# Neighbourhood heads: each block of 64 queries against its own 128 keys, its values gathered by 16 transfers from GpSimd

## The reference

```
ncb = GRID_W // NA_COL_BLOCK                        # 4 blocks of 16 columns
kstart = clip(arange(ncb) * 16 - 8, 0, 64 - 32)     # 0, 8, 24, 32
kcol = kstart[:, None] + arange(32)                 # 32 key columns for each block
wstart = clip(qcol - 8, 0, 64 - 16)
col_valid = (kcol >= wstart) & (kcol < wstart + 16)
sc = einsum('bnqhd,banchd->bhnqac', qb, kb) * scale + bias
sc = where(col_valid, sc, -inf)
p = softmax(sc, axis=(-2, -1))
o = einsum('bhnqac,banchd->bnqhd', p, vb)
```

## Time and profile before

| | us |
|---|---|
| median of 3 | 1472.59 (1472.44 to 1472.97) |
| profiled execution | 1472.36 |
| its span | 1471.1 |
| TensorE products busy | 1449.6 |
| VectorE busy | 1043.9 |
| ScalarE busy | 815.8 |
| GpSimd busy | 62.4 |

### The profile page before, as it was taken

The page is one execution under the profiler, slowest core; times in us unless marked ns, Lnnn a source line. Parts: engine busy times, 40 slices in busy tenths (PEclk is TensorE's granted clock), DMA queues, the critical chain, the costliest instruction groups (busy, mean ns, idle before and its releaser), DMA issues.

```text
span 1471.1 us, 19474 instructions
## 1 busy us (share of the span) xinstructions
PE 1449.6 (99%) x7635; PEld 1215.1 (83%) x7635; DVE 1043.9 (71%) x1409; ACT 815.8 (55%) x1159; POOL 62.4 (4%) x100
## 2 busy tenths in 40 slices
PE   7999999999999999999999999999999999999998
PEld 5788887888888788887888888788888888888887
DVE  5656885865567656786866555877988868788886
ACT  3565654444544455754445444686665557775563
POOL 2000000000000000000010000210000012000000
PEclk9999999999999999999999999999999999999999
DMA  9553643566566535543666665336556635356651
GB/s 322 182 162 127 237 169 115 191 229 200 172 193 207 194 103 183 186 139 125 196 203 201 198 202 201 115 115 208 169 196 198 225 119 172 125 182 201 200 181 58
DMA packets 167324, 261.08 MB, mean 177 GB/s; under 512 B 8768, under 2 KB 106720, under 8 KB 166720
## 3 DMA queue, kind: packets, MB, share of 16 engines
q1 hardware_dynamic: 166048, 252.03, 52.0%
q0 software_dynamic: 896, 6.74, 1.2%
q10 hardware_dynamic: 288, 1.05, 0.2%
HBM read 258.74 MB, written 1.05 MB: 177 GB/s over the span
## 4 chain that ended last, share of the span: by engine, by line
PE 85%; DVE 9%; ACT 3%; issue 1%; POOL 1%; DMA 1%; SPq 0%; DVEq 0%; ACTq 0%
PE ps L421 16%; PE ps L492 10%; PE ps L494 10%; PE ps L493 10%; PE ps L422 9%; PE ps L391 6%; PE ps L395 6%; PE ps L393 6%; DVE wlo L1581 3%; PE ps L424 2%; PE ps L546 1%; PE ps L559 1%; PE ps L569 1%; PE ps L449 1%; DVE x L1600 1%
## 5 line engine op out<-in xcount | busy, mean ns | idle before, releaser
L1581 DVE TENSOR_TENSOR wlo<-raw,whi 128x2048 fp32r<-128x2048 f32 (+1 forms) x238 | 528.3, 2229 | 224.7 <-ACT whi L1097 224.7
L1097 ACT ACTIVATE whi<-raw 128x2048 fp32r<-128x2048 f32 (+1 forms) x238 | 441.9, 1866 | 152.2 <-PE ps L494 54.3
L421 PE MATMUL ps<-xT,whi 128*128 128x512 f32 x1008 | 356.4, 395 | 0.0
L422 PE MATMUL ps<-xT,wlo 128*128 128x256 f32 x1152 | 311.2, 280 | 0.0
L492 PE MATMUL ps<-whi,xT 128*128 128x512 f32 (+3 forms) x640 | 250.6, 391 | 4.3 <-DVE xT L1619 2.3
L494 PE MATMUL ps<-whi,xT 128*128 128x512 f32 (+3 forms) x640 | 242.0, 378 | 0.0
L493 PE MATMUL ps<-wlo,xT 128*128 128x512 f32 (+3 forms) x640 | 241.4, 377 | 0.0
L421 PEld LDWEIGHTS ps<-xT,whi 128*128 128x128 f32 x1008 | 189.0, 188 | 42.2
L422 PEld LDWEIGHTS ps<-xT,wlo 128*128 128x128 f32 x1152 | 217.4, 189 | 6.1
L492 PEld LDWEIGHTS ps<-whi,xT 128*128 128x128 f32 x640 | 120.4, 188 | 29.9 <-issue 7.8
L494 PEld LDWEIGHTS ps<-whi,xT 128*128 128x128 f32 x640 | 120.2, 188 | 22.6
(11 more groups left out here) (220 smaller groups left out, 1962.0 us busy)
## 6 DMA issues: line engine op xcount, KB each, us to landing
raw<-in_w_in SPq DMA_DIRECT2D x124, 512.0 KB, 4.7
raw<-in_w_ffn_in SPq DMA_DIRECT2D x88, 512.0 KB, 4.9
raw<-in_w_up SPq DMA_DIRECT2D x88, 512.0 KB, 4.8
raw<-in_w_ffn_out SPq DMA_DIRECT2D x44, 512.0 KB, 4.4
raw<-in_w_down SPq DMA_DIRECT2D x44, 512.0 KB, 4.4
raw<-in_w_branch SPq DMA_DIRECT2D x24, 512.0 KB, 4.6
raw<-in_w_out SPq DMA_DIRECT2D x16, 512.0 KB, 4.5
raw<-in_w_o SPq DMA_DIRECT2D x16, 512.0 KB, 4.7
```

What stands on the lines that cost most here:

```text
L421: PE.matmul(ps[:, b, :], hi, m.xT[:, kt], start=kt == 0, stop=False)
L422: mm = PE.matmul(ps[:, b, 0:S], lo, m.xTh[:, kt], start=False, stop=False)
L1097: AC.activation(m.whi[:, i % SPLIT, 0:w], m.raw[:, slot, 0:w], ACT.Copy).then_inc(s.w_hi, 1)
L1581: DV.tensor_tensor(m.wlo[:, i % SPLIT, 0:w], m.raw[:, slot, 0:w], m.whi[:, i % SPLIT, 0:w].bitcast(F32), ALU.subtract).then_inc(s.w_lo, 1)
```

## The change

Queries and keys are put in another order, so that the 64 queries of one block are neighbours, and each block is scored against its own 128 keys. The scores of a head are then 2 x 128 columns in place of 2 x 256. The queries are reordered when they are copied out of PSUM, the keys are picked by an access pattern, and the bias is laid out to fit on the host: `rpb` holds 128 columns for each half and head, 1 MB in rows of 128 elements. In the free half of `rpb` four tiles of values are put together, one for each block: 16 transfers from SBUF to SBUF, which GpSimd starts once the values are out of PSUM. TensorE waits for them ahead of the first product with values. The results are put back in the order of the tokens when they are copied out.

```
+WINDOWS = (0, 8, 24, 32)
...
     def load_bias(L):
-        PO.dma_start(m.rpb[:], t["rpb"][L]).then_inc(s.lay, 16)
+        PO.dma_start(m.rpb[:, :, :, 0:P], t["rpb"][L]).then_inc(s.lay, 16)
...
         PO.dma_start(m.vec[:], t["b_gate"][L:L + 1, 0:2 * D].broadcast_to([P, 2 * D])).then_inc(s.gate_b, 16)
+        for th in range(2):
+            bank, nth = k.bank[(1, L, "n", 2), th]
+            PO.wait_ge(k.free[bank], nth)
+        for w, k0 in enumerate(WINDOWS):
+            for r in range(4):
+                p0 = r % 2 * 64 + k0
+                PO.dma_start(m.rpb[32 * r:32 * r + 32, 2 * w:2 * w + 2, :, P:S],
+                             m.proj[p0:p0 + 32, r // 2, 1024:1536].rearrange("p (a b e) -> p a b e", a=2, b=2)).then_inc(s.windows_in, 16)
...
+    def score_windows(g0, h0, g):
+        PE.wait_ge(s.qk_out, g0 + g + 1)
+        if h0 + g:
+            PE.wait_ge(s.exped, h0 + 2 * g)
+        for w, k0 in enumerate(WINDOWS):
+            half, b = w // 2, w % 2
+            for j in range(2):
+                qk = m.qk[64 * j:64 * j + 64, g % 2, :]
+                keys = qk[:, S:2 * S].rearrange("p (r c) -> p r c", r=4)[:, :, k0:k0 + 32]
+                mm = PE.matmul(ps[64 * b:64 * b + 64, 3 + j, half * P:(half + 1) * P], qk[:, w * 64:w * 64 + 64], keys,
+                               start=True, stop=True)
+                if w == 3:
+                    mm.then_inc(s.scored, 1)
+    def turn_windows(p0, i, buf):
...
+        for half in range(2):
+            mm = PE.transpose(ps[:, 5, half * P:(half + 1) * P], m.prob[:, buf, half, 0:P], m.ident[:])
+        mm.then_inc(s.probs_turned, 1)
+    def mix_windows(p0, m0, g):
...
+        for w in range(4):
+            for j in range(2):
+                values = m.rpb[:, 2 * w + g // 2, g % 2, P + 64 * j:P + 64 * j + 64]
+                o = (g % 2) * S + 64 * w
+                mm = PE.matmul(ps[64 * j:64 * j + 64, 7, o:o + 64], values, m.probT[:, j, 64 * w:64 * w + 64],
+                               start=True, stop=True)
+        mm.then_inc(s.pairs_mixed, 1)
...
             if g == 1:
-                out_of_psum((1, L, "n", 2))
+                PE.wait_ge(s.windows_in, 256 * (L + 1))
             if g:
-                mix_pair(p0, m0, g - 1, 1024)
+                mix_windows(p0, m0, g - 1)
...
-        AC.activation(m.probT[:, i % 2, :], ps[:, 5, :], ACT.Copy).then_inc(s.probs_out, 1)
+        AC.activation(m.probT[:, i % 2, 0:width], ps[:, 5, 0:width], ACT.Copy).then_inc(s.probs_out, 1)
...
+    def qk_by_columns(buf):
+        DV.wait_ge(s.qk_turned, n.up("groups"))
+        DV.tensor_copy(columns(m.qk[:, buf, 0:S]), by_columns(ps[:, 6, 0:S]))
+        DV.tensor_copy(m.qk[:, buf, S:2 * S], ps[:, 6, S:2 * S]).then_inc(s.qk_out, 1)
...
-                b = DV.tensor_tensor_reduce(m.prob[:, h % 4, th, :], ps[:, 3 + h % 2, th * S:(th + 1) * S], m.rpb[:, h, th, :], 1.0,
+                b = DV.tensor_tensor_reduce(m.prob[:, h % 4, th, 0:P], ps[:, 3 + h % 2, th * P:(th + 1) * P], m.rpb[:, h, th, 0:P], 1.0,
```

More of the change, by code:

```diff
@@ L60 @@
     "gate_tanh", "merged",
-    "rotated", "subln", "lam", "lam_exp",
+    "windows_in", "rotated", "subln", "lam", "lam_exp",
     "qk_turned", "qk_out", "scored", "negm", "exped", "heads_out",
@@ L121, in gemm_names, with by_columns, columns @@
     return seq
+def by_columns(ap):
+    return ap.rearrange("p (r w c) -> p w r c", r=4, w=4)
+def columns(ap):
+    return ap.rearrange("p (w r c) -> p w r c", r=4, w=4)
 def spread(ap, shape, axis=1):
@@ L549, in score_pair @@
                     mm.then_inc(s.scored, 1)
+    def score_windows(g0, h0, g):
[12 more added lines that the diff above has]
+    def turn_windows(p0, i, buf):
+        PE.wait_ge(s.probs_in, p0 + i + 1)
+        if p0 + i:
+            PE.wait_ge(s.probs_out, p0 + i)
+        for half in range(2):
+            mm = PE.transpose(ps[:, 5, half * P:(half + 1) * P], m.prob[:, buf, half, 0:P], m.ident[:])
+        mm.then_inc(s.probs_turned, 1)
+    def mix_windows(p0, m0, g):
+        PE.wait_ge(s.probs_out, p0 + 2 * g + 2)
+        if m0 + g:
+            PE.wait_ge(s.pair_out, m0 + g)
+        for w in range(4):
[5 more added lines that the diff above has]
+        mm.then_inc(s.pairs_mixed, 1)
     def turn_probs(p0, i, buf):
@@ L640, in tensor_program @@
             if g < 4:
-                score_pair(g0, h0, g)
+                score_windows(g0, h0, g)
             if g < 3:
@@ L645, in tensor_program @@
             if g:
-                turn_probs(p0, 2 * g - 2, (2 * g - 2) % 4)
+                turn_windows(p0, 2 * g - 2, (2 * g - 2) % 4)
             fill(g, 2)
             if g:
-                turn_probs(p0, 2 * g - 1, (2 * g - 1) % 4)
+                turn_windows(p0, 2 * g - 1, (2 * g - 1) % 4)
             fill(g, 3)
             if g == 1:
-                out_of_psum((1, L, "n", 2))
+                PE.wait_ge(s.windows_in, 256 * (L + 1))
             if g:
-                mix_pair(p0, m0, g - 1, 1024)
+                mix_windows(p0, m0, g - 1)
         fill(5, 0, rest=True)
@@ L1206, in exp_pair, with probs_out @@
             for th in range(2):
-                src = m.prob[:, h % 4, th, :] if biased else ps[:, 3 + h % 2, th * S:(th + 1) * S]
-                e = AC.activation(m.prob[:, h % 4, th, :], src, ACT.Exp, bias=m.negm[:, h % 4, 1, th:th + 1], scale=scale,
+                dst = m.prob[:, h % 4, th, 0:P if biased else S]
+                src = dst if biased else ps[:, 3 + h % 2, th * S:(th + 1) * S]
+                e = AC.activation(dst, src, ACT.Exp, bias=m.negm[:, h % 4, 1, th:th + 1], scale=scale,
                                   accum_out=m.rs[:, h, th:th + 1])
             e.then_inc(s.exped, 1)
-    def probs_out(p0, i, m_free):
+    def probs_out(p0, i, m_free, width=2 * S):
         AC.wait_ge(s.probs_turned, p0 + i + 1)
@@ L1220, in pair_hi, with windows_hi @@
         AC.activation(m.aTh[:, g, :], ps[:, 7, (g % 2) * S:(g % 2 + 1) * S], ACT.Copy).then_inc(s.pair_hi, 1)
+    def windows_hi(m0, g):
+        AC.wait_ge(s.pairs_mixed, m0 + g + 1)
+        AC.activation(by_columns(m.aTh[:, g, :]), columns(ps[:, 7, (g % 2) * S:(g % 2 + 1) * S]), ACT.Copy).then_inc(s.pair_hi, 1)
     def outputs_hi(kts, bank):
@@ L1275, in scalar_program @@
             if g:
-                probs_out(p0, 2 * g - 2, m0 + g - 1)
+                probs_out(p0, 2 * g - 2, m0 + g - 1, S)
             catch(1, L, "na", g, 2, ahead=SPLIT - (g > 2))
             if g:
-                probs_out(p0, 2 * g - 1, m0 + g - 1)
+                probs_out(p0, 2 * g - 1, m0 + g - 1, S)
             catch(1, L, "na", g, 3)
             if g:
-                pair_hi(m0, g - 1)
+                windows_hi(m0, g - 1)
         catch(1, L, "na", 5, 0)
@@ L1763, in biased_maxima, with normalise_pair @@
             DV.tensor_scalar(m.negm[:, h % 4, 1, :], m.negm[:, h % 4, 0, :], -1.0, None, ALU.mult).then_inc(s.negm, 1)
-    def normalise_pair(h0, g):
+    def normalise_pair(h0, g, width=S):
         DV.wait_ge(s.exped, h0 + 2 * g + 2)
@@ L1769, in normalise_pair @@
             for th in range(2):
-                p = m.prob[:, h % 4, th, :]
+                p = m.prob[:, h % 4, th, 0:width]
                 a = DV.tensor_scalar(p, p, m.ri[:, h, th:th + 1], None, ALU.mult)
@@ L1789, in pair_lo, with windows_lo @@
                          ALU.subtract).then_inc(s.pair_out, 1)
+    def windows_lo(g):
+        DV.wait_ge(s.pair_hi, n.up("pair_hi"))
+        DV.tensor_tensor(by_columns(m.aTl[:, g, :]), columns(ps[:, 7, (g % 2) * S:(g % 2 + 1) * S]),
+                         by_columns(m.aTh[:, g, :].bitcast(F32)), ALU.subtract).then_inc(s.pair_out, 1)
     def blocks_lo(lo, hi, nkt, bank0, koff=0, gain=None):
@@ L1852, in vector_program @@
         h0, p0 = n.up("heads", 8) - 8, n.up("probs", 8) - 8
-        qk_out(P, 0)
+        qk_by_columns(0)
         catch(1, L, "na", 0, 0, ahead=SPLIT - 1)
@@ L1856, in vector_program @@
             if g in (1, 2, 3):
-                normalise_pair(h0, g - 1)
+                normalise_pair(h0, g - 1, P)
             if g < 4:
@@ L1860, in vector_program @@
             if g < 3:
-                qk_out(P, (g + 1) % 2)
+                qk_by_columns((g + 1) % 2)
             catch(1, L, "na", g, 1, ahead=0 if g else SPLIT)
             if g == 3:
-                normalise_pair(h0, g)
+                normalise_pair(h0, g, P)
             if g == 1:
@@ L1873, in vector_program @@
             if g:
-                pair_lo(g - 1)
+                windows_lo(g - 1)
         catch(1, L, "na", 5, 0)
@@ L2262, in rpb_rows @@
     a = np.where(inside[None, None, None, :, None, :], a, np.float32(-1e30))
-    return a.reshape(DEPTH, 8, 2, P, S).transpose(0, 3, 1, 2, 4)
+    window = 2 * np.arange(2)[:, None] + np.arange(P) // 64
+    column = 16 * window + np.arange(P) % 16
+    keys = np.array(WINDOWS)[window][:, :, None] + np.arange(P) % 32
```

(2 more changed lines are left out.)

## The result

| us | before | changed |
|---|---|---|
| median | 1472.51 (1472.27 to 1472.97, 4 runs) | 1461.72 (1461.69 to 1461.87, 4 runs) |
| profiled execution, span | 1472.36, 1471.1 | 1461.71, 1460.4 |
| TensorE products busy | 1449.6 | 1438.3 |

The ratio is 0.9927, 95% interval [0.9915, 0.9939]: 10.8 us faster. The forecast was 6.1 faster, and its range ended at 1462.0, just above the measured time.

What follows compares the result with a forecast made beforehand. TensorE's program was taken to bound the kernel: 1472.36 less 8.1 us for shorter scores, values and transposes, plus 2.1 for a late bias, gave 1466.4 us. The range was 1462.0 to 1474.0.

Steps and rivals of the forecast that it cites:

- TensorE is the path, and what it saves counts in full: Whole kernel: TensorE, busy 99% of the span, sets the time; an instruction taken out of it counts in full.
- Transposes, 0.43 a pair: Neighbourhood heads: transposes go from eight to four per pair of heads, saving 0.43 us a pair.
- Scores and values, taken at 0.75 us each: Neighbourhood heads: score and value blocks fall from 1.07 and 1.01 to 0.75 us, saving 0.32 and 0.26 a pair.
- all quarters at once: Score and value blocks: four array quarters run together, 0.61 us per block, saving 1.29 a pair, 10.3 in all.
- The price of an instruction (d): Score and value blocks: TensorE pays 0.107 us per instruction, not for columns; 1484.3 us with the bias, chance 0.10.
- The bias, priced by the row, +2.1: Layer 0: issuing the bias's 2048 rows takes 8.7 us, so VectorE runs late and TensorE waits 2.1 us, once.
- The other bound: Layer 0 bias: an issue costs the same, 0.6 us, and half the data lands sooner; gain nothing.
- the slack: Layer 0: VectorE's first `wlo` ends at 40.8 and TensorE uses it at 41.13, 0.3 us to spare.
- Sixteen transfers, hidden by 1.8 us: Transfers of values: 0.55 us an issue, landed by 68.4, 1.8 us before the product at 70.2; cost 0 in both layers.
- The cousin: VectorE's three `wlo` hold up the sixteen issues, which land 1.2 us late, twice: 1468.8 us, chance 0.05.
- Everything off the path, 0: VectorE and ScalarE: shorter maxima, exponentials, normalisation and copies cover nothing TensorE waits for; 0.
- rival (a): Layer 0: the bias lands no later than before; 1464.3 us, down to 1462.1 with all quarters side by side; chance 0.22.

Runs made afterwards that it cites:

- two_quarters: The changed kernel with all score products written to PSUM partitions 0 to 63, so on two of the array's four quarters: 1465.18 us.
- one_half: The changed kernel with both heads' products with the values on the same half of the array: 1465.27 us.
- bias_4096_rows: The changed kernel with the bias transferred twice, 2 x 2048 rows, the second into the free half of its tile: 1469.74 us.
- old_widths: The changed kernel with ScalarE copying 512 columns of turned probabilities and VectorE normalising 256, as before the change: 1462.22 us.

## Why the prediction was too cautious

- **TensorE is the path, and what it saves counts in full.** Right: 10.3 us of shorter blocks, 10.65 us between the two profiled executions, nothing taken back later.
- **Transposes, 0.43 a pair.** Right: 0.21 twice in the trace, 3.9 us when undone.
- **Scores and values, taken at 0.75 us each.** This step failed: the saving was sized too small. I had worked out 0.61 for all quarters at once and then took a value "nearer to the first", to be safe between ends of 0.61 and 1.01. They measured 0.60 and 0.61. The way of counting was right: rounds of moving columns over the parts of the array in use, plus 0.16. At 0.75 the sum has 8.1 us where 10.3 came, 2.2 of the 4.7 by which the time was off. `two_quarters` shows that the scores' share comes from the quarters side by side, and `one_half` that the values' columns count on each half; that the 0.16 is a change of the array's shape is not shown. For the quarters the Trainium skill, "TensorEngine Tiling (Array Packing)", Key Properties, was the better guide: tiles load and multiply in parallel, and 1.02 us became 0.60 by that alone. Between bounds that differ by whether a thing works, the middle is no forecast: one end or the other comes.
- **The price of an instruction (d).** It is there, 0.028 us in the mean of two halves, 0.058 on each. The 0.107 of the earlier trace rows was no bound on it: those instructions have twice the stationary columns and the whole array to themselves. The values' block stops shrinking just where this change leaves it; the scores' is not shown to. The rule of some 60 cycles a matmul, which the prediction cited against the change from the Trainium skill ("TensorEngine Tiling (Array Packing)", Instruction Overhead), is an estimated 0.025 us at 2.4 GHz. The run agrees in kind, 32 columns cost what 64 do; in size it does for the mean of 0.028, and not for the 0.058 on one half.
- **The bias, priced by the row, +2.1.** This step failed. I multiplied 0.55 us for 128 rows by 16, to 8.7; it was 1.36. From 128 to 2048 rows the issue grew by 0.62, 0.3 ns a row. VectorE went on at 36.5, not 40.4, and TensorE had no wait. A price that is the same for long and short rows was read as a price for rows, when it was a price for the transfer. Rows do cost when two such transfers follow each other: in `bias_4096_rows` the second starts only once the first has landed. The other bound (same cost, half the data, landing sooner) was nearly exact; the slack and the path behind it were right too, as `bias_4096_rows` shows.
- **Sixteen transfers, hidden by 1.8 us.** Right in the outcome: 0.54 an issue, started at 55.20, the product at 70.06. The margin was smaller than I had it: the last of them landed at 68.90 in layer 0, 1.2 ahead of the product, and at 516.89 in layer 1, 1.0 ahead. I took landings of 3.9 to 4.9 from single transfers; sixteen in a row took up to 6.1. The cousin, VectorE holding up the issues, did not happen: the seven that begin beside three `wlo` in a row took 549 to 574 ns, and all 32 took 549 to 592. The Trainium skill tells of its lock ("SBUF — State Buffer", section SBUF: two separate sides) for VectorE's two-port operations; an operation with two inputs from SBUF, as the subtraction of `wlo` is, contends by the page only with a GpSimd operation that reads SBUF. So the prediction was wrong to put the time at the cousin's by this rule. The trace agrees with the page as far as it goes: neither `wlo` nor what followed it up to 64 us delayed an issue.
- **Everything off the path, 0.** Right but for ScalarE's narrower copy ahead of the first product with values, worth the half microsecond of `old_widths`.

In sum, 4.7 = 2.2 (blocks) + 2.1 (bias) + some 0.4, of which 0.2 is the shorter wait for the probabilities in layer 1; the rest is rounding. The case that came is rival (a) with all quarters side by side, which I had at 1462.1 and at the edge of the range.

## What to carry to other kernels

Where TensorE is the path, count a block of small products as moving columns per part of the array in use, plus some 0.15 us for the block as a whole. On two halves, believe it down to a mean of 0.03 us an instruction. Products that lie on different rows or different columns of the array run side by side: the scores took 0.60 us so and 1.02 on the same columns. Cut in two on the same columns, they gain hardly anything, 1.02 against the 1.07 of before.

Price the issue of a transfer from GpSimd by the transfer, 0.55 us, and little by rows (1.36 for 2048), but do not put two of 2048 rows behind each other. Keep the last landing ahead of its use: a wait of 5 us on TensorE costs some 2 us more behind it, in a halved clock.

## What the runs showed that I had not expected

- Two transfers of 2048 rows did not start back to back: the second stood 10.8 and 7.7 us behind the first with no semaphore between, each time 0.3 us behind the first's landing, while three of 128 rows each followed a large one in 0.55 us steps, and sixteen of 128 rows followed each other without a gap.
- A single wait of TensorE of 5.8 us cost about 8: for 4.0 us behind it the granted clock was 0.50, with plain products 0.63 us long and 0.43 apart.
